# Two heads that share their values in one product of 256 columns: attention of a two-layer hybrid backbone on one core

## What is computed

```python
# A and B: 8 query heads, 2 key/value heads (G = 4 query heads share one); N: 8 and 8
s = jnp.einsum('bqkgd,bskd->bkgqs', qi, keys) * ATTN_SCALE
p = jax.nn.softmax(s, axis=-1)
o = jnp.einsum('bkgqs,bskd->bqkgd', p, vals)
```

## Time and profile before

| | us |
|---|---|
| median of 3 runs | 1580.23 |
| the three runs | 1577.54, 1580.23, 1580.57 |
| the profiled execution, its own time | 1584.0 |
| its span | 1582.2 |
| TensorE busy in the span | 1526.1 (96%) |
| VectorE busy | 706.7 (45%) |
| ScalarE busy | 367.9 (23%) |
| GpSimd busy | 144.2 (9%) |

### The profile page before, as it was taken

One profiled execution on the slowest core, in us unless ns is written; L12 is line 12 of the kernel. 1 busy time (PEld: TensorE's weight loads), 2 busy tenths in 40 slices (PEclk: granted clock), 3 DMA queues, 4 the chain that ended last, 5 costly groups with the idle time before them and its releaser, 6 DMA issues. The chain is left out here.

```text
span 1582.2 us, 18774 instructions
## 1 busy us (share of the span) xinstructions
PE 1526.1 (96%) x7202; PEld 816.1 (52%) x7202; DVE 706.7 (45%) x1508; ACT 367.9 (23%) x878; POOL 144.2 (9%) x233
## 2 busy tenths in 40 slices
PE   8999999999999999999999989999999999989897
PEld 4478766667776646644333334456644445333332
DVE  2356278789994344511111246206776236111113
ACT  3022288811111111111111023107810011000001
POOL 1100001200000100001021220000300010101010
PEclk9999999999999998999999999999999998999999
DMA  9823240124844473489999996442169667999987
GB/s 334 269 54 107 71 133 5 38 82 134 284 149 175 150 293 117 179 300 401 371 417 419 378 339 189 151 179 69 41 168 388 245 240 272 388 406 412 411 353 288
DMA packets 110186, 371.88 MB, mean 235 GB/s; under 512 B 25616, under 2 KB 29856, under 8 KB 93540
## 3 DMA queue, kind: packets, MB, share of 16 engines
q1 hardware_dynamic: 96688, 332.42, 56.5%
q0 software_dynamic: 12976, 37.95, 6.9%
q10 hardware_dynamic: 432, 0.29, 0.1%
HBM read 363.20 MB, written 19.73 MB: 242 GB/s over the span
## 5 line engine op out<-in xcount | busy, mean ns | idle before, releaser
L2914 PE MATMUL bank<-ring_sb,HT_sb 128*64 128x512 f32 x544 | 122.0, 601 | 1.3 <-ACT HT_sb L1387 0.7
L2499 PE MATMUL bank<-ring_sb,HT_sb 128*128 128x512 f32 x256 | 115.0, 605 | 2.5 <-ACT HT_sb L1123 2.5
L1513 DVE SCALAR_TENSOR_TENSOR MB_sb<-ring_sb,cT_sb,MB_sb 128x512 f32<-128x512 f32 x144 | 108.3, 752 | 5.1
L2951 PE MATMUL bank<-ring_sb,QR_sb 128*64 128x512 f32 x336 | 80.3, 622 | 17.7 <-DMA ring_sb<-w_e_down 15.2
L2608 PE MATMUL bank<-QR_sb,ring_sb 128*128 128x512 f32 x192 | 86.3, 592 | 0.0
L2580 PE MATMUL bank<-ring_sb,HT_sb 128*128 128x512 f32 x192 | 85.4, 595 | 0.8 <-issue 0.8
L2185 DVE TENSOR_TENSOR QR_sb<-QR_sb,bank 64x512 f32<-64x512 f32 x21 | 21.9, 1044 | 139.4 <-ACT QR_sb L1403 139.4
L2499 PEld LDWEIGHTS bank<-ring_sb,HT_sb 128*128 128x128 f32 x256 | 48.9, 194 | 63.2 <-issue 63.2
L2914 PEld LDWEIGHTS bank<-ring_sb,HT_sb 128*64 128x64 f32 x544 | 38.9, 138 | 73.1 <-issue 71.9
L2651 PE MATMUL bank<-KR_sb,QR_sb 64*128 64x512 f32 (+1 forms) x288 | 70.5, 568 | 3.9 <-ACT MB_sb L1325 2.9
L2622 PEld LDWEIGHTS bank<-tab_sb,MB_sb 128*128 128x128 f32 x480 | 51.4, 141 | 43.9 <-issue 41.3
(11 more groups left out here) (446 smaller groups left out, 2481.5 us busy)
## 6 DMA issues: line engine op xcount, KB each, us to landing
ring_sb<-w_e_down SPq DMA_DIRECT2D x32, 2048.0 KB, 17.1
ring_sb<-w_mod SPq DMA_DIRECT2D x24, 2048.0 KB, 10.8
ring_sb<-w_in SPq DMA_DIRECT2D x21, 2048.0 KB, 17.7
ring_sb<-w_e_gate SPq DMA_DIRECT2D x16, 2048.0 KB, 11.5
ring_sb<-w_e_up SPq DMA_DIRECT2D x16, 2048.0 KB, 16.7
ring_sb<-w_e_gate SPq DMA_DIRECT2D x22, 1024.0 KB, 17.1
ring_sb<-w_e_up SPq DMA_DIRECT2D x22, 1024.0 KB, 19.4
ring_sb<-w_branch SPq DMA_DIRECT2D x8, 1024.0 KB, 13.1
```

What stands on the lines that cost most here:

```text
L1513: link(stt(a, WR[slot][:, k], cT[:, k, strm:strm + 1], a, ALU.mult, ALU.add))
L2499: ins = mm(bank[j % 4][:, :], HT[:, k, P * t:P * t + P], WR[slot][:, k], start=(k == 0), stop=(k == KD - 1))
L2914: ins = mm(bank[0][HALF * side:HALF * side + HALF, :], hgT[q % 2][:, k, 0:HALF], w[k], start=(k == 0), stop=(k == KD - 1))
L2951: ins = mm(bank[4][HALF * half:HALF * half + HALF, :], eaT[:, k, 0:HALF], w[k][:, CW * half:CW * half + CW], start=(k == 0), stop=(k == 3))
```

## The change

The value products of pairs 2i and 2i+1 are issued together, in the step of the second. In A and B one product takes the transposed probabilities of both pairs as 256 moving columns; in N the two pairs' products keep their 128 columns and stand in one group. The two sides of `PT` grow to 1024 columns each, in two buffers: the first lies where both old ones lay (half in `WK`, half in `MB`), the second in layer 0 in ring slot 5 and in layer 1 in `X`'s context tiles. So `g01` can be loaded into slot 5 only when layer 0's last value products are done, and its load goes behind the biases.

```diff
-            order.append((key, slot, last[slot], last[slot] in late))
+            order.append((key, slot, last[slot], last[slot] in late or last[slot] == ("sums", 0)))
...
-        PT = [[W[:, at + CW * side:at + CW * (side + 1)].rearrange("p (k q) -> p k q", k=4) for side in range(2)]
-              for W, at in ((WK, D + SEQ), (MB, 3 * D + 8))]
+        PT = [[[v.rearrange("p (k j q) -> p k j q", k=4, j=2) for v in pair] for pair in (
+            (WK[:, D + SEQ:2 * D + SEQ], MB[:, 3 * D + 8:4 * D + 8]), second)] for second in (
+                tuple(ring[:, SUMS].rearrange("p a b -> p (a b)")[:, D * i:D * i + D] for i in range(2)),
+                tuple(X[:, NLAT + i] for i in range(2)))]
...
             if key[0] == "sums":
-                return whole, 3 * GROUPS
+                return pv_mm, len(att_pairs(0))
...
-                        if d >= 2:
-                            eng.wait_ge(pv_mm, p - 1)
+                        if d >= 4:
+                            eng.wait_ge(pv_mm, 2 * (p // 2) - 2)
                         for side in range(2):
                             eng.wait_ge(pt_tr, 2 * p + side + 1)
-                            act(PT[p % 2][side][:, ks], bank[3 + side][:, :].rearrange("p (k q) -> p k q", k=4)[:, ks],
+                            act(PT[l][p // 2 % 2][side][:, ks, j % 2], bank[3 + side][:, :].rearrange("p (k q) -> p k q", k=4)[:, ks],
                                 ACT.Copy).then_inc(pt_copied, 1)
...
-                    if 0 <= d < M:
+                    if 0 <= d < M and d % 2:
...
                         eng.wait_ge(pt_copied, 2 * p + 2)
-                        if j == 0 and g >= 2:
+                        if j == 1 and g >= 2:
                             eng.wait_ge(o_copied, g - 1)
-                        for k in ks:
-                            for side in range(2):
-                                h = head(b, j, side)
-                                v = vN[:, k, DH * h:DH * h + DH] if b == N else \
-                                    vAB[:, k, b, DH * side:DH * side + DH]
-                                dst = bank[5 + g % 2][DH * side:DH * side + DH, P * j:P * j + P]
-                                ins = mm(dst, v, PT[p % 2][side][:, k], start=(k == ks[0]), stop=(k == NT - 1))
-                        ins.then_inc(pv_mm, 1)
+                        for jj in range(2 if b == N else 1):
+                            for k in ks:
+                                for side in range(2):
+                                    part = slice(DH * side, DH * side + DH)
+                                    now = PT[l][p // 2 % 2][side][:, k]
+                                    if b == N:
+                                        h = head(b, j - 1 + jj, side)
+                                        ins = mm(bank[5 + g % 2][part, P * (j - 1 + jj):P * (j + jj)],
+                                                 vN[:, k, DH * h:DH * h + DH], now[:, jj],
+                                                 start=(k == ks[0]), stop=(k == NT - 1))
+                                    else:
+                                        ins = mm(bank[5 + g % 2][part, P * (j - 1):P * (j + 1)],
+                                                 vAB[:, k, b, part], now, start=(k == ks[0]), stop=(k == NT - 1))
+                        ins.then_inc(pv_mm, 2)
```

## The result

The changed kernel takes 1582.77 us (median, 1579.41 to 1588.29), the kernel before beside it on the same chips 1579.26 us (1574.31 to 1583.6). The profiled execution took 1587.42 us, its span is 1585.7 us.

What follows compares the result with a forecast made beforehand. TensorE was taken to bound attention; 6.2 us of saved group starts, 6.0 us of stalls and 0.7 us beside GpSimd gave +0.5 us on 1580.23, about 1580.7 us, range 1576.3 to 1584.5.

Steps and rivals of the forecast that it cites:

- the likeliest case: Whole kernel: +0.5 us, about 1580.7 us, no change within 0.2%; layer 0 loses about 1 us; chance 0.62.
- the stalls: Attention: long steps' transposes wait on VectorE's scaling or ScalarE's copies that short steps no longer cover; 6.0 us lost.
- the three bounds: Uncertainties around the forecast time: group 0.8 us, GpSimd's biases 0.8 us, a third of the stalls either way 2 us.
- What bounds attention: Attention in both layers: TensorE is the limit, with nothing idle between groups, at a granted clock of 1.00.
- The group starts: Attention on TensorE: double groups of 1.87, 1.01 and 1.91 us save 6.2 us, 4.1 in layer 0, 2.1 in layer 1.
- rival 3: Value products: the group start stays, only single matmuls' fixed part goes, 0 to 1 us saved; 1586 us, chance 0.06.
- GpSimd's neighbourhood: Branch N: scaling beside GpSimd's bias work takes longer, up to 0.21 us per first half; 0.7 us counted.
- The release to TensorE adds 0.06: Long steps' transposes: TensorE starts 0.06 us after VectorE's scaling ends, added to each VectorE chain.
- Layer 1 gain about 1.1 us: Layer 1's attention: 2.1 us of saved group starts against 1.0 us of stalls.
- Rival 2: Long steps' transposes: VectorE's chain outlasts the cover by 0.1 us in A latent too; 5.1 us, 1586 us, chance 0.1.
- Copies with gaps, `g01`, larger buffers: Copies out of transpose banks, g01's later load and PT buffer waits: each counted as costing nothing.
- That what attention loses shifts all that follows, one for one: After attention: whatever it gains or loses moves the merge and everything later by the same amount.

Runs made afterwards that it cites:

- the new order: Changed kernel, but in every second step VectorE scales the even pair before the odd pair's row maxima; 1577.83 us, ratio 0.9996.
- the new order alone: Kernel before, with VectorE scaling two pairs in odd steps and none in even ones, nothing else changed; 1580.46 us, ratio 1.0001.
- Pair by pair: Changed kernel with value products issued per pair again, 128 columns each, keeping larger buffers, gapped copies and late g01 load; 1580.4 us, ratio 1.0003.

## Why the prediction was right, and where it was off

The time lay in the range, and the likeliest case had the right mechanism and the right sign in layer 0 (in layer 1 the measured 0.2 us is no more than two profiles of one kernel differ by): forecast +0.5 us, measured 1.0024, or 3.5 us between the medians. That is past the 0.2% within which the forecast saw no change, so the likeliest case's number did not come true. (Its upper end, given as 1583.4, is +3.2 us; the three bounds added straight give 1584.3.) Attention is 2.0 us longer because the stalls were undersized. The rest, 1.5 us or more, lies outside attention; the interval's lower end, 1.0013, would leave nothing for it.

**What bounds attention** stood: TensorE, with nothing idle before the change, at a clock of 1.00.

**The group starts** (6.2 us saved) were right, term by term: 1.88, 1.02 and 1.90 us for 1.87, 1.01 and 1.91. Layer 1 confirms the sum without its stalls: with the new order attention there is 2.2 to 2.3 us shorter, for 2.1 forecast. The Trainium skill's "TensorE: Matmul & The Clock Gate", section "Back-to-back issue gap", whose formula for an isolated matmul has a fixed 2.5 ns, would by an estimate have given 0.8 us (rival 3). These rows, and the run with 128 columns (half as many columns a product, almost the same group), put the price at the change of kind of group instead.

**The stalls** (6.0 us, with 0.7 for GpSimd's neighbourhood) were in the right places and too small. Taken from start to start, less the scores' own 1.06 or 0.64 us:

| wait of the long step's transposes | forecast | measured |
|---|---|---|
| A latent | 0 | 0.05 |
| A context | 0.12 | 0.24 |
| B latent | 0.18 | 0.30 |
| B context | 0.37 | 0.50 |
| N latent | 0.08 | 0.16 to 0.59 |
| N context | 0.12 | 0.24 |
| latent to context (A, B, N) | 0.35, 0.61, 0.51 | 0.46, 0.72, 0.58 |
| context to latent (B, N) | 0.61, 0.51 | 0.74, 0.63 |
| ScalarE's copies after the first context step | 0.25 | 0.23 |

Nearly every wait on VectorE is 0.12 us over its forecast; the one on ScalarE is not. The step that failed is "The release to TensorE adds 0.06", together with half of the pair's row as the first scaling. The chain in A, context queries, of the changed kernel:

```profile
222.03 0.76 DVE L1849 TENSOR_REDUCE nmx_sb<-bank 128x1 f32<-128x256 f32 x2 [1.49 <-PE bank L2659]
...
222.90 0.62 DVE L1835 TENSOR_SCALAR MB_sb<-MB_sb,rcp_sb 128x256 f32<-128x256 f32 x2
...
223.37 0.34 PEld L2624 LDWEIGHTS bank<-tab_sb,MB_sb 128*128 128x128 f32 x3 [0.55 <-ACT MB_sb L1310]
...
223.40 0.41 PE L2624 MATMUL bank<-tab_sb,MB_sb 128*128 128x128 f32 x2 [0.17 <-DVE MB_sb L1835]
```

From the scaling's start to the transposes are 223.40 - 222.90 = 0.50 us, where I had 0.31 + 0.06 = 0.37. A lone scaling of that size, cut out of the pair, is recorded with

```profile
226.83 0.35 DVE L1835 TENSOR_SCALAR MB_sb<-MB_sb,rcp_sb 128x256 f32<-128x256 f32 x1
```

so 0.04 of the difference is the half (two in a row overlap in their records), and 0.09 the release: scaling done at 223.25, weight load at 223.37, first transpose at 223.40, 0.15 us in all. The 0.06 of the earlier trace rows was taken where TensorE waited for the *second* side's scaling, with the first side's transposes done. In B's latent steps it is the same: scaling from 240.78, transposes at 241.42, 0.64 us for a forecast of 0.44 + 0.06 = 0.50.

The profile before the change had the right row, in branch B, where latent steps begin:

```profile
237.32 0.88 DVE L1833 TENSOR_SCALAR MB_sb<-MB_sb,rcp_sb 128x512 f32<-128x512 f32 x2
...
237.96 1.06 PE L2622 MATMUL bank<-tab_sb,MB_sb 128*128 128x128 f32 x8
```

From the scaling's start to the transposes it is 0.64 us as well. Read there, the term would have been right.

Put back into the sum for layer 0: some 15 waits on VectorE with 0.13 us more each are 2.0 us. Forecast 5.1, so 7.1; the starts add up to 7.3. The kernel before had about 0.9 us of such waits, which fall into these. 7.1 - 0.9 - 4.1 = 2.1 us slower, measured 2.1. That it comes out so well is partly luck, for two terms that neither the forecast nor this sum counts nearly cancel. The transposes at 313.78, behind the last scores, wait 0.6 us for a scaling that VectorE does after work of the merge. And a group of transposes that has waited takes 0.03 us less (0.99 for 1.02, 0.56 for 0.59), 17 times, 0.5 us. In layer 1 seven waits more by 0.13 bring 1.0 to 1.9 us, GpSimd's neighbourhood 0.6; the starts add up to 2.6. Less 0.2 for waits of the kernel before and 0.2 for the shorter transposes, that is 2.2 against 2.1 saved: nothing left, measured 0.2 gained. "Layer 1 gain about 1.1 us" failed on the same term.

**Rival 2**, that transposes would wait on VectorE by 0.1 us more than counted, was therefore the side on which I erred: its surplus came to pass, in B, N and context steps. In A's latent steps, its deciding point, it did not (0.05 us), and so it brought 2 us and not 5.

**GpSimd beside the scaling** (0.7 us) is real and was read too small: of the 1.31 us of the earlier trace rows the first scaling alone takes 0.91, 0.42 more than without GpSimd, and not 0.21. The wait of 0.59 is such a place:

```profile
1134.45 1.31 DVE L1835 TENSOR_SCALAR MB_sb<-MB_sb,rcp_sb 128x512 f32<-128x512 f32 x2
...
1135.51 1.07 PE L2624 MATMUL bank<-tab_sb,MB_sb 128*128 128x128 f32 x8 [0.53 <-DVE MB_sb L1835]
```

From the scaling's start to the transposes are 1.06 us here and 0.64 elsewhere. It met two of the five latent waits within N, with 0.2 and 0.4 us, so that the total of 0.7 us came near by fewer and larger ones. GpSimd has a second way to cost time that the forecast left out: VectorE's maxima in N wait for its biases (up to 0.17 us in the changed kernel, 0.88 in the kernel before, 1.87 with the new order alone). No run takes either alone.

**Copies with gaps, `g01`, larger buffers** (nothing): right. Pair by pair the ratio is 1.0003 with attention at 131.1 and 83.2. `g01` goes out at 320.59, where the forecast had it,

```profile
320.59 0.37 SPq L730 DMA_DIRECT2D ring_sb<-w_in  x1
```

lands 9.0 us later, at 329.61, long before 345, and merge 0 is 232.6 us in all eleven profiles.

**That what attention loses shifts all that follows, one for one**, holds in layer 0's merge, and not further on. Attention accounts for 2.0 to 2.2 us, a ratio of 1.0013; measured is 1.0024. In the profiles layer 1's merge is longer by 3.8 us, and by 0.8 us in the second pair of them (126.7 and 126.6 us against 122.9 and 125.8), for the landing of the weight load shown above and the clock behind it. The kernel before shows that wait too, and the run with the new order, whose attention is 2.7 us shorter than before, shows the longest. Whether the change makes the long form more frequent, and so whether the rest of the measured time is the change's, is open: two profiles of each kernel can't tell.

## What to carry to other kernels

Joining two short groups of matmuls saved the start of one here, whatever the width of the products in it; but it makes steps uneven, and every hand-over between engines that an even step had hidden must then fit into the short one. Read each hand-over at the place where it will decide (for the first operand of a group, with the weight load in it), since 0.13 us too little in a term that occurs 22 times is 2.9 us, more than the 2.0 us that attention lost. When a step becomes uneven, let the engine that feeds it do its work for two steps at once, ahead of what can wait: here this brought back 2.5 and 2.2 us of attention, where neither the grouping nor that order alone brought more than 0.2. None of these variants is shown to be faster than the kernel before: every interval of theirs holds 1.

## What the runs showed of the hardware

A value that VectorE writes reaches a waiting group of transposes 0.12 us (weight load) to 0.15 us (first transpose) after the write's recorded end, while for a later operand, with the group's first transposes done, shows 0.06 us. In the eleven profiles every release of a group's first transposes by a scaling takes 0.15 us, and every one of later transposes 0.06. (The wait at 259.45 in the changed kernel is put down to a scaling, 0.05 us after it, but ends with ScalarE's copies, which are done at 259.40.)

After a wait of 2 to 3 us between busy stretches the granted clock can fall for a while. Two stretches of 10 us from 1190 on, of the kernel before in its first profile:

```profile
1190.00:1200.00 10.00, 9.19 (x28) 3.57 (x27) 0.89 (x2) 0.00 (x0) 0.50 (x1) 1.00 1.05 386
1200.00:1210.00 10.00, 10.00 (x25) 4.39 (x24) 9.55 (x15) 0.60 (x1) 0.50 (x1) 1.00 1.05 387
```

of the changed kernel, where the wait is 2.94 us:

```profile
1190.00:1200.00 10.00, 7.06 (x22) 2.51 (x21) 0.99 (x2) 0.60 (x1) 0.50 (x1) 0.95 1.05 373
1200.00:1210.00 10.00, 10.00 (x22) 4.37 (x21) 6.43 (x9) 0.60 (x1) 0.00 (x0) 0.88 1.05 387
```

and of the kernel before again, with a wait of 2.08 us:

```profile
1190.00:1200.00 10.00, 7.92 (x21) 2.88 (x21) 0.69 (x1) 0.00 (x0) 0.50 (x1) 0.83 1.05 386
```

A mean of 0.83 or 0.88 over 10 us means that part of them ran at the 1.2 GHz level: in the last of these profiles the sixteen matmuls after the wait take 8.74 us in place of 7.10. Behind waits of 0.81, 1.34, 1.90 (twice) and 2.09 us the clock stayed at 1.00, behind those of 2.03, 2.08, 2.42, 2.82, 2.94 and 3.22 it did not. So a wait costs its own length, and sometimes half as much again and more behind it.

A scaling by VectorE of 128x512 elements takes 0.49 us by itself and 0.91 us beside GpSimd's work on the biases, which is under way for most of it (0.63 us of the 0.91, before 1135.36).
